# First attention block: the probabilities are scaled by VectorE instead of the outputs by products that spread the reciprocals

## The reference, cut to what matters

```python
p = sink_softmax(jnp.concatenate([s_win, s_ctx], axis=-1)).astype(vw.dtype)
return (jnp.einsum('bgrls,bsgd->blgrd', p[..., :SPAN], vw)
        + jnp.einsum('bgrls,bsgd->blgrd', p[..., SPAN:SPAN + n_ctx], v_c))
```

## Time and profile before

| | |
|---|---|
| Time, median of 3 runs | 4044.75 us (4042.74 to 4045.05) |
| The profiled execution's own time | 4049.56 us |
| Its span | 4047.8 us, 47201 instructions |
| Mean granted clock of TensorE | 0.988 of full speed |
| Busy in the span | TensorE 96%, its weight loads 60%, VectorE 54%, ScalarE 21%, GpSimd 15% |
| Stage of the first attention | from about 176 to 397 us of the span |

### The profile page before, as it was taken

One profiled execution on the slowest core, in us unless ns is written; L12 is line 12 of the kernel. 1 busy time (PEld: TensorE's weight loads), 2 busy tenths in 40 slices (PEclk: granted clock), 3 DMA queues, 4 the chain that ended last, 5 costly groups with the idle time before them and its releaser, 6 DMA issues.

```text
span 4047.8 us, 47201 instructions
## 1 busy us (share of the span) xinstructions
PE 3896.3 (96%) x18130; PEld 2414.5 (60%) x18130; DVE 2185.3 (54%) x3630; ACT 838.5 (21%) x1655; POOL 594.1 (15%) x944
## 2 busy tenths in 40 slices
PE   8999999999999999999999998899999999999998
PEld 5677588844455555548744645655555444758863
DVE  0254532356566556434466015737777765437886
ACT  1266111100112312212101113521100012531000
POOL 1000000033213422400132002200000430000023
PEclk9999999999999999999999998999999999999999
DMA  5255011244412222312344212411112552002234
GB/s 188 102 193 196 21 62 53 86 175 171 156 45 91 78 80 94 105 63 92 117 167 155 73 42 78 156 53 61 53 62 67 173 177 70 18 22 84 88 130 161
DMA packets 209788, 410.67 MB, mean 101 GB/s; under 512 B 5938, under 2 KB 92296, under 8 KB 209440
## 3 DMA queue, kind: packets, MB, share of 16 engines
q1 hardware_dynamic: 203712, 386.94, 28.1%
q0 software_dynamic: 5856, 20.73, 1.6%
HBM read 405.49 MB, written 2.16 MB: 101 GB/s over the span
## 4 chain that ended last, share of the span: by engine, by line
PE 90%; DVE 5%; ACT 3%; DMA 1%; issue 1%; POOL 0%; DVEq 0%; ACTq 0%; SPq 0%; POOLq 0%
PE PS L1212 25%; PE PS L1330 19%; PE PS L1172 5%; PE PS L1145 3%; PE PS L1812 3%; PE PS L1123 3%; PE PS L1266 3%; PE PS L1826 3%; PE PS L915 2%; PE PS L1813 1%; PE PS L1973 1%; PE PS L1983 1%; PE PS L1457 1%; PE PS L1426 1%; PE PS L1125 1%; PE PS L1082 1%
## 5 line engine op out<-in xcount | busy, mean ns | idle before, releaser
L1212 PE MATMUL PS<-UT,RING 128*128 128x256 f32 (+1 forms) x2432 | 640.5, 411 | 10.2 <-ACT BIG L3037 8.8
L1212 PEld LDWEIGHTS PS<-UT,RING 128*128 128x128 f32 x2432 | 461.7, 190 | 151.1 <-issue 13.9
L1212 PE MATMUL PS<-BIG,RING 128*128 128x256 f32 (+1 forms) x1824 | 487.7, 410 | 0.8 <-DVE BIG L2872 0.5
L1212 PEld LDWEIGHTS PS<-BIG,RING 128*128 128x128 f32 x1824 | 345.9, 190 | 106.5 <-DVEq L2048 1.5
L1330 PE MATMUL PS<-RING,BIG 128*128 128x512 f32 x810 | 376.8, 593 | 2.2 <-ACT UT L2997 1.4
L3649 POOL TENSOR_TENSOR RES_TMP<-BIG 128x128 f32<-128x128 f32 x68 | 35.6, 524 | 1689.9 <-DVE BIG L2878 583.0
L1330 PEld LDWEIGHTS PS<-RING,BIG 128*128 128x128 f32 x810 | 151.4, 190 | 181.8 <-issue 176.8
L2723 DVE TENSOR_TENSOR RING<-RING 128x512 f32<-128x512 f32 x135 | 105.8, 784 | 273.6 <-DMA RING<-ff_w_dram 168.1
L1330 PE MATMUL PS<-RING,GATE 128*128 128x512 f32 x536 | 243.3, 595 | 5.2 <-DVE RING L2726 5.2
L1330 PE MATMUL PS<-RING,RES_TMP 128*128 128x512 f32 x544 | 245.2, 593 | 0.6 <-DVE RING L2726 0.6
L1330 PEld LDWEIGHTS PS<-RING,GATE 128*128 128x128 f32 x536 | 102.2, 191 | 135.1 <-issue 125.4
(11 more groups left out here) (472 smaller groups left out, 6021.6 us busy)
## 6 DMA issues: line engine op xcount, KB each, us to landing
RING<-ff_w_dram SPq DMA_DIRECT2D x112, 1024.0 KB, 5.0
RING<-w_mod_dram SPq DMA_DIRECT2D x48, 2048.0 KB, 8.1
RING<-w_ffn_down_dram SPq DMA_DIRECT2D x55, 1024.0 KB, 5.0
RING<-w_ffn_up_dram SPq DMA_DIRECT2D x44, 1024.0 KB, 5.1
RING<-ssm_w_in_dram SPq DMA_DIRECT2D x8, 2048.0 KB, 8.0
RING<-ssm_w_out_dram SPq DMA_DIRECT2D x4, 2048.0 KB, 8.5
RING<-w_even_in_dram SPq DMA_DIRECT2D x4, 2048.0 KB, 8.3
GATE<-gates_dram POOLq DMA_DIRECT2D x12, 512.0 KB, 7.8
```

The costliest lines, as they stand in the source:

```text
L1212: m = mm(bank(bank_, n), a[:, k, :], b[:, k, :], start=k == 0, stop=k == 3)
```

## The change

TensorE no longer makes the products that spread the reciprocals, and where a unit has no third group of pieces, it has no third turn either. VectorE, behind the reciprocals of unit p in step p+1, multiplies each head's exponentials in place with that head's reciprocal, and posts `unit_probs_normed`; TensorE's transposes of unit p, in step p+2, wait for that instead of `probs_ready`. The output is copied as it is. ScalarE copies only the pieces of the third group, where there is one.

```diff
--- before.py
+++ after.py
@@ -747,11 +747,7 @@
                 pieces = self.pieces()
                 return pieces[0:4], pieces[4:8], pieces[8:]
 
-            def spread_at(self):
-
-                return self.tiles * len(self.heads) * 128
-
-            def spread_width(self):
+            def out_width(self):
 
                 return len(self.heads) // 2 * 128
 
@@ -1430,7 +1426,7 @@
                     p = s_ - 2
                     if 0 <= p < n:
                         first, second_, _ = UNITS[p].groups()
-                        pe.wait_ge(S("probs_ready"), p + 1)
+                        pe.wait_ge(S("unit_probs_normed"), p + 1)
                         for part in (first, second_):
                             _, m = turn(p, part)
                             m.then_inc(tf.full, 1)
@@ -1441,8 +1437,6 @@
                         for i, (j, h) in enumerate(pieces):
                             if i % 4 == 0:
                                 pe.wait_ge(tf.free, tf.slots + copied[s_ - 3][i // 4])
-                            if i == len(pieces) - 1:
-                                pe.wait_ge(tf.free, tf.slots + copied[s_ - 3][2])
                             half = h % 2 * 64
                             o = x + h // 2 * 128
                             m = mm(PS[half:half + 64, o:o + 128], q.values[h][j], A_PT[:, (s_ - 3) % 2, i * 128:(i + 1) * 128],
@@ -1458,18 +1452,8 @@
                             if i == one:
                                 m.then_inc(S("bank_sharer_scored"), 1)
                     m.then_inc(sf.full, 1)
-                    if 0 <= p < n:
-                        _, _, last = UNITS[p].groups()
-                        if last:
-                            b, _ = turn(p, last)
-                        else:
-                            b = 6 + place(tf)
-                            copied[p].append(taken[tf])
-                        pe.wait_ge(S("unit_reciprocals_ready"), p + 1)
-                        for h in range(len(UNITS[p].heads)):
-                            half = h % 2 * 64
-                            m = mm(bank(b, 128, (len(last) + h // 2) * 128)[half:half + 64, :],
-                                   unit_reciprocals(p)[:, h:h + 1].to_broadcast([128, 64]), ident, start=True, stop=True)
+                    if 0 <= p < n and UNITS[p].groups()[2]:
+                        _, m = turn(p, UNITS[p].groups()[2])
                         m.then_inc(tf.full, 1)
                     if s_ in MOD_STEPS:
                         mod_rows(*MOD_STEPS[s_], 6 + place(tf), alone=False)
@@ -2239,9 +2223,7 @@
                     dve.wait_ge(sf.full, s_ + 1)
                     if s_ >= 3:
                         q = UNITS[s_ - 3]
-                        w, a = q.spread_width(), q.spread_at()
-                        step(V.tensor_tensor(q.out(), PS[:, x:x + w].rearrange("p (c l) -> p c l", l=128),
-                                             A_PT[:, (s_ - 3) % 2, a:a + w].rearrange("p (c l) -> p c l", l=128), ALU.mult))
+                        step(V.tensor_copy(q.out(), PS[:, x:x + q.out_width()].rearrange("p (c l) -> p c l", l=128)))
                     if s_ < n:
                         u = UNITS[s_]
                         if u.windows:
@@ -2263,7 +2245,12 @@
                         dve.wait_ge(S("unit_sums_ready"), p + 1)
                         step(V.tensor_tensor(unit_reciprocals(p), unit_sums(p), unit_sinks(p), ALU.add))
                         step(V.reciprocal(unit_reciprocals(p), unit_reciprocals(p)))
-                        post("unit_reciprocals_ready")
+                        w = UNITS[p].width
+                        for h in range(len(UNITS[p].heads)):
+                            probs = A_P[:, p % 2, h * w:(h + 1) * w]
+                            step.go(V.tensor_scalar(probs, probs, unit_reciprocals(p)[:, h:h + 1], None, ALU.mult))
+                        step.settle()
+                        post("unit_probs_normed")
 
             def mixer0():
                 g, r = flow(0, "v", NT), flow(0, "rot", 2)
@@ -3201,8 +3188,8 @@
 
                         act.wait_ge(S("maxima_ready"), s_)
                         post_free(sf)
-                    if 0 <= p < n:
-                        w = 128 * len(UNITS[p].groups()[2]) + UNITS[p].spread_width()
+                    if 0 <= p < n and UNITS[p].groups()[2]:
+                        w = 128 * len(UNITS[p].groups()[2])
                         ready(tf)
                         give(tf, A(A_PT[:, p % 2, 1024:1024 + w], bank(6 + uses % 2, w), ACT.Copy))
                         uses += 1
```

## The result

The changed kernel takes 4197.05 us (median of 4 runs, 4194.57 to 4197.26), the kernel before beside it 4043.89 us (median of 4). The ratio is 1.0374, with a 95% interval of 1.0361 to 1.0387: 153 us slower. The forecast was 4190 us.

A forecast was written before the change was run, and what follows sets the result against it. The prediction took TensorE to bound the kernel and the stage of the first attention. Loops 94.7 us more, about 2 each at start and end, sum 99; with 46 for the clock, 4044.75 + 145 = 4190 us; 8 in 10: 4130 to 4250.

The forecast's parts named there:

- The loop: First attention: VectorE's and TensorE's legs no longer overlap but follow each other; 38 loops take 300.1 us, 94.7 us more.
- The first condition: List of waits: transposes wait behind VectorE some 39 times, about 2 us after modulation steps, 4 us after others.
- The scaling: VectorE, behind the reciprocals: multiplying the exponentials takes 1.07, 0.95 and 1.33 us per inner, edge and context unit.
- the upper bound: Scaling at the two-input product's pace, about 0.83 us for 640 elements: the stage 15 us more.
- The handover: From VectorE's last scaling to TensorE: estimated 0.15 us, each 0.1 us of it worth 4 us of the stage.
- The removed products: TensorE, first attention: some 15 us of products spreading the reciprocals go, but are worth nothing where TensorE will idle.
- The clock: TensorE's legs after long idle time run slow for four fifths: 43 us, with others 46 us more.
- the main forecast: Clock low in part of TensorE's legs in the first attention: 4190 us, chance 0.50.
- the rival with nearly all legs slow: Idle time behind modulation steps also lowers TensorE's clock: 38 x 2.8 = 106 us, so 4250 us; chance 0.19.
- The rival in which the clock holds: First attention: TensorE's clock doesn't fall, the legs' lost overlap alone costs time: 4144 us; chance 0.23.
- The start and the end: First attention: the first and last units wait for their scaling with nothing else to do, about 2 us each.
- The not-slower rival: VectorE's idle time takes the scaling before the next scores; only some 15 us gain is left: 4030 us; chance 0.02.

The follow-up runs named there:

- the kernel that holds the clock: Changed kernel with 6 identity products nobody reads added to TensorE's steps with modulation, 13 to the others: 4146.63 us, ratio 1.0248.
- the run with the wait alone: Changed kernel without its scalings, the transposes still waiting for VectorE's post behind the reciprocals: 4128.96 us, ratio 1.0208.
- the first filler run: Changed kernel with 10 identity products nobody reads added to TensorE's steps with modulation, 24 to the others: 4176.18 us, ratio 1.0325.

## Why the prediction was right

**The loop closed as forecast.** The first condition, 39 waits of the transposes behind VectorE, shows as 40. Over the prediction's 38 loops VectorE's legs were forecast at 164.8 us and measured at 159.8; TensorE's at full clock were forecast at 135.3 us, and the kernel that holds the clock shows 136.6, at the lengths of the working (3.75 us for 3.73, 3.54 for 3.50, 3.55 for 3.52). In that kernel the loops take 91 us more than before, for 94.7 forecast; the output projection starts 97 us later, and the whole takes 100 us more, where the sum said 99. That 100 and 99 are so close is in part luck: 3 of the 100 us lie outside the stage, and the added products lengthen its start and end from 3 to 6 us.

**The scaling** was priced on the line between two rows at 1.07, 0.95 and 1.33 us per unit, and took 1.02, 0.90 and 1.14. (The line itself gives 0.01 us more per scaling than the working has; it changes nothing.) The slower pace of the two-input product, the upper bound, isn't there: 551 ns for 640 elements, not 830. The handover that was put at 0.15 us took 271.70 - 271.59 = 0.11. The first is worth 3.0 us over the 38 loops and the second 1.5, together most of the 5 us by which VectorE's legs came out short.

**The removed products** were said to be worth nothing in the loop, as they lie beside VectorE's leg. Shown by the pair of runs with the wait moved, with and without products. In the open pipeline they are worth 16 us within the stage and 18 in all, where the working had 15.

**The clock** was the uncertain term: 46 us forecast, 51 measured. That its size came out near is in part luck, since two errors partly cancel. The slow legs cost less than the 2.8 us at which they were priced from rows wholly at 1.2 GHz: 2.2 us in long gaps and 1.6 in short ones, since in most the clock comes back before the leg ends; but there are more of them: all 18 legs with scores behind long gaps where the working had four fifths of 19, some 39 us for 43, and eight of the legs behind modulation besides, some 13 us. The step that took the others as fast, at a few us, is where the sum was off, by some 10 us. The mean clock was off too: the sign for the main forecast was about 0.85, for the rival with nearly all legs slow under 0.75, and the stage shows 0.78, between them. The rival in which the clock holds (4144 us) is what the run with fewer added products shows as 4146.6; it wasn't what happened. The rival with nearly all legs slow throughout (4250 us) fails on the two counts just named: eleven of the 19 legs behind modulation stayed fast, and no leg was slow from end to end to the measure of 6.7 us. The Trainium skill ("TensorE: Matmul & The Clock Gate", section "HAM oscillation — how this bites in real kernels") describes a kernel in which each wait of about 3 to 5 us for a DMA leaves the burst behind it to start throttled; it doesn't say so of every wait. In the changed kernel's trace it is so for the legs behind 2.7 us of idle time and more, so also behind shorter waits than in that example, and not for those behind 2.10 us and less.

**The start and the end** of the stage were put at about 2 us each. Step 2, from which the loops are counted, starts 0.9 us later than before (186.94 against 186.09 us). From the start of step 40 to the output projection it is 8.99 us (537.01 to 546.00) instead of 6.42 (391.45 to 397.87), 2.6 us more. Together that is 3.4 us for the 4 forecast. With the loops, 350.1 us instead of 205.4, it makes the 148 us of the stage; the other 5 of the 153 lie outside the stage or between executions.

**The not-slower rival** had its deciding place right, the order in VectorE's queue, and its price wrong: with the scaling ahead, the result is not 4030 but 4086 us, as a loop through ScalarE takes over. I had overlooked in the prediction that the sums of a unit come only when the scores of the next are nearly done; the order in the queue alone already excluded this rival.

## What to carry to other kernels

In a software pipeline, ask of each added wait how many steps lie between the producer and the consumer, and what is queued ahead of the producer on its engine: 40 us of work that is free beside the path closed a loop that cost 100 us when one step too few lay between, and went with a gain of 19 us with one step and one buffer more. An engine that is half idle is no proof of room for work that is waited for. And price a wait on TensorE twice, once for its length and once for the products behind it, which may run at 1.2 GHz: here that was 51 of 153 us.

## What the runs showed of the hardware

Idle time of TensorE that ends in a fall of the clock isn't of one length. Behind 2.60 us in the run with the wait moved and the products kept, legs came out at 5.33 and at 3.75 us in the same stretch. Behind 3.12 us in the run with the wait alone, two inner legs took 3.75 us and the others 5.4 to 6.5. And shorter idle time than the 2.10 us behind which the changed kernel's legs are fast can be enough: in the run with the products kept, transposes of the context behind 1.90 us took 1.97 us, and their leg 4.92 instead of 3.55. A fast leg of the run with the wait alone, and this slow one of the run with the products kept:

```profile
360.57 1.09 PE L1422 MATMUL PS<-CS,BIG 128*128 128x128 f32 x8 [3.12 <-DVEq L2032]
...
448.21 1.97 PE L1426 MATMUL PS<-CS,BIG 128*128 128x128 f32 x8 [1.90 <-DVEq L2048]
```

Adding work to an engine made the kernel 50 us faster.

The added products of the identity followed each other at 0.11 to 0.12 us per record, two records each (26 in 3.07 us), while the records of the values' products, with as many moving columns but only 64 columns of weights, follow at 0.06 us (20 from 271.04 to 272.28 us in the first filler run), and those of the modulation products with 32 at 0.03 us (64 in 1.95 us). I hadn't expected that. Whether the width of the weights does it is open, since it wasn't tried by itself; the values' products also write in turn to the lower and the upper 64 rows of PSUM, and the modulation products to four groups of 32 rows, so neighbours may overlap for that reason.
